# Thirty-six short extra products on TensorE ahead of weight chunks of the feed-forward layers

## The reference

```python
x = x + 0.5 * g1 * swiglu(modulate(x, sh1, sc1), ffn1_gate[l], ffn1_up[l], ffn1_down[l])
x = x + g2 * token_mix(modulate(x, sh2, sc2), ...)          # two kinds of attention
x = x + 0.5 * g3 * swiglu(modulate(x, sh3, sc3), ffn2_gate[l], ffn2_up[l], ffn2_down[l])
# swiglu(u) = (silu(u @ w_gate) * (u @ w_up)) @ w_down, width D_FF = 2816 = 22 * 128
```

## Time and profile before

| | us |
|---|---|
| median of 3 runs | 2264.29 |
| lowest and highest run | 2263.94, 2271.13 |
| span of the profiled execution, first to last instruction | 2258.5 |
| median less that span | 5.8 |
| TensorE (PE) busy | 2177.8 |
| VectorE (DVE) busy | 1526.8 |
| ScalarE (ACT) busy | 1182.8 |

### The profile page before, as it was taken

How to read it: one execution, slowest core, us unless ns; L and a number is a source line. 1 busy time by engine, 2 the same in 40 slices (tenths; PEclk the granted TensorE clock), 3 DMA queues, 4 the chain that set the end, 5 groups by cost and what they waited for, 6 DMA issues and landing times.

```text
span 2258.5 us, 40704 instructions
## 1 busy us (share of the span) xinstructions
PE 2177.8 (96%) x16754; PEld 1932.4 (86%) x16754; DVE 1526.8 (68%) x2122; ACT 1182.8 (52%) x2059; POOL 369.9 (16%) x360
## 2 busy tenths in 40 slices
PE   7999999999999999999999999999999988999998
PEld 7888988988888889988888988788878978868887
DVE  6897767688778866767775874387557544626753
ACT  4554557565455544765554664365446431526542
POOL 0111022111102100311111103020232350303001
PEclk9999999999999999999999999999998999999999
DMA  7887662467768768434665443355524300434552
GB/s 277 328 308 252 242 244 94 149 236 259 243 232 295 274 214 315 161 103 165 214 223 186 166 159 130 131 170 186 177 91 150 103 4 12 160 129 146 190 186 95
DMA packets 114232, 417.79 MB, mean 185 GB/s; under 512 B 12672, under 2 KB 12928, under 8 KB 113664
## 3 DMA queue, kind: packets, MB, share of 16 engines
q1 hardware_dynamic: 113184, 410.34, 52.2%
q10 hardware_dynamic: 864, 4.84, 0.6%
HBM read 414.09 MB, written 1.05 MB: 184 GB/s over the span
## 4 chain that ended last, share of the span: by engine, by line
PE 81%; DVE 7%; ACT 5%; issue 4%; POOL 1%; DMA 1%; POOLq 0%; SPq 0%; DVEq 0%; ACTq 0%
PE banks L551 80%; DVE weight_lower L1520 1%; DVE weight_ring L1531 1%; POOL heap L2718 1%; ACT weight_upper L2230 1%; ACT xn_t L2354 1%; PE banks L954 1%; PE banks L1340 0%; DMA weight_ring<-w_ada_dram 0%; ACT L2264 0%; ACT xn_t L2277 0%; DMA weight_ring<-w_in_dram 0%; ACT heap L2387 0%; DMA weight_ring<-ffn_up_dram 0%; ACT xn_halves L2245 0%
## 5 line engine op out<-in xcount | busy, mean ns | idle before, releaser
L551 PE MATMUL banks<-xn_halves,weight_upper 128*128 128x512 f32 (+1 forms) x3680 | 1004.8, 344 | 11.3 <-DVE weight_lower L1520 8.1
L1520 DVE TENSOR_TENSOR weight_lower<-weight_ring,weight_upper 128x1024 fp32r<-128x1024 f32 x580 | 743.1, 1287 | 315.4 <-ACT weight_upper L2230 314.2
L551 PE MATMUL banks<-xn_halves,weight_lower 128*128 128x256 f32 x2832 | 802.0, 283 | 6.6 <-DVE xn_halves L1553 2.9
L2230 ACT ACTIVATE weight_upper<-weight_ring 128x1024 fp32r<-128x1024 f32 x580 | 607.9, 1054 | 351.7 <-PE banks L551 202.6
L551 PEld LDWEIGHTS banks<-xn_halves,weight_upper 128*128 128x128 f32 x3680 | 637.6, 190 | 99.5 <-issue 7.9
L551 PEld LDWEIGHTS banks<-xn_halves,weight_lower 128*128 128x128 f32 x2832 | 538.6, 190 | 9.9 <-DVE xn_halves L1553 3.2
L551 PE MATMUL banks<-hidden,weight_upper 128*128 128x512 f32 x1216 | 430.0, 397 | 0.0
L551 PE MATMUL banks<-hidden,weight_lower 128*128 128x256 f32 x1216 | 341.7, 281 | 0.0
L551 PEld LDWEIGHTS banks<-hidden,weight_upper 128*128 128x128 f32 x1216 | 228.6, 188 | 56.4
L2718 POOL TENSOR_TENSOR heap<-heap 128x256 f32<-128x256 f32 x120 | 122.0, 1021 | 930.5 <-ACT heap L2460 614.5
L551 PEld LDWEIGHTS banks<-hidden,weight_lower 128*128 128x128 f32 x1216 | 228.2, 188 | 0.0
(11 more groups left out here) (299 smaller groups left out, 2496.1 us busy)
## 6 DMA issues: line engine op xcount, KB each, us to landing
weight_ring<-w_ada_dram SPq DMA_DIRECT2D x144, 512.0 KB, 4.5
weight_ring<-ffn_gate_dram SPq DMA_DIRECT2D x88, 512.0 KB, 3.8
weight_ring<-ffn_up_dram SPq DMA_DIRECT2D x88, 512.0 KB, 4.5
weight_ring<-ffn_down_dram SPq DMA_DIRECT2D x88, 512.0 KB, 3.4
weight_ring<-m_w_up_dram SPq DMA_DIRECT2D x64, 512.0 KB, 3.2
weight_ring<-m_w_down_dram SPq DMA_DIRECT2D x64, 512.0 KB, 3.2
weight_ring<-w_in_dram SPq DMA_DIRECT2D x58, 512.0 KB, 4.0
weight_ring<-b_w_rkv_dram SPq DMA_DIRECT2D x24, 512.0 KB, 3.2
```

The lines of the kernel that those rows point to most:

```text
L551: return nc.tensor.matmul(o, w, r, start=first, stop=last)
L1520: V.tensor_tensor(w_lo[:, n % RING, :], ring[:, n % RING, :], w_hi[:, j % SPLITS, :].bitcast(F32), ALU.subtract).then_inc(*did("weight_low ...
L2230: A.activation(w_hi[:, j % SPLITS, :], ring[:, n % RING, :], ACT.Copy).then_inc(*did("weight_upper", j))
```

## The change

In stages 2 and 5, ahead of the gate chunk of `f` = 4, 7, 10, 13, 16 and 19, and in the way down of all four feed-forward stages, ahead of chunks 4, 7, 10, 13, 16 and 19, TensorE gets an extra product (in one case two) into PSUM bank 5, whose result nobody reads. Its kind varies from place to place. It stands behind the chunk's wait in `cut` and ahead of the chunk's first pair. Nothing else is changed, and all that the kernel computed before it still computes.

```diff
+NUDGES = {(2, 4): "narrow", (2, 7): "tile", (2, 10): "two", (2, 13): "split", (2, 16): "short", (2, 19): "wide",
+          (5, 4): "half", (5, 7): "quarter", (5, 10): "turn", (5, 13): "wide", (5, 16): "narrow", (5, 19): "split"}
+DOWN_NUDGES = {4: "narrow", 7: "tile", 10: "split", 13: "turn", 16: "wide", 19: "short"}
...
+            def nudge(kind, w):
+
+                refill(5)
+                if kind == "narrow":
+                    mm(cols(5, 1), ident, ident[:, 0:1], True, True)
+                elif kind == "tile":
+                    mm(cols(5, P), ident, ident, True, True)
+                elif kind == "two":
+                    for _ in range(2):
+                        mm(cols(5, P), ident, ident, True, True)
+                elif kind == "half":
+                    mm(cols(5, 64), ident, ident[:, 0:64], True, True)
+                elif kind == "quarter":
+                    mm(cols(5, 32), ident, ident[:, 0:32], True, True)
+                elif kind == "turn":
+                    nc.tensor.transpose(cols(5, P), ident, ident)
+                elif kind == "split":
+                    mm(cols(5), w[0][:, 0:P], xn_hl[0][:, 0, :], True, True)
+                elif kind == "short":
+                    mm(cols(5, P), w[0][:, 0:P], xn_hl[0][:, 0, 0:P], True, True)
+                elif kind == "wide":
+                    mm(bank[:, 5, :].rearrange("p (h t) -> p h t", h=2), w[0][:, 0:P], xn_hl.both[:, :, 0, :],
+                       True, True)
...
-            def project_wide(name, i, x, done, readers_of, b):
+            def project_wide(name, i, x, done, readers_of, b, kind=None):
...
                 w, *used = cut(name, i)
+                nudge(kind, w)
                 for k in range(KD):
...
                             wc, *used = cut(name, i0 + m // TILES)
+                            if kt == KF and m // TILES in DOWN_NUDGES:
+                                nudge(DOWN_NUDGES[m // TILES], wc)
...
-                        project_wide(name, i, xn_hl, done, readers_of, b)
+                        project_wide(name, i, xn_hl, done, readers_of, b,
+                                     NUDGES.get((s, f)) if name.endswith("gate") else None)
```

## The result

The changed kernel takes 2272.14 us, median of 18 runs, beside 2264.01 for the kernel before in 18 runs of the same sets. The recorded ratio of the two is 1.0044, 95% interval [1.0031, 1.0058]: slower by 9.9 us, between 7.0 and 13.1. (It is not the quotient of the medians; these differ by 8.1 us, and the means by 9.6.) The forecast was 2267.3 within 2261 to 2274, that is 3.0 us slower. The time lies in the range; the loss is three times the forecast one, and it fell to the case of slower by over 0.3%, which had 0.19.

What follows compares the result with a forecast made beforehand. TensorE, running without a stop, was taken to bound the kernel. Products cost 4.9 us, quicker gate stretches return 1.9, net 3.0 more: span 2261.5, plus 5.8 to the median, 2267.3 us, range 2261 to 2274.

Steps and rivals of the forecast that it cites:

- the case of slower by over 0.3%: Whole kernel: a loss above 0.3%, 6.8 us; chance 0.19.
- What bounds the kernel: Stretches concerned: TensorE runs without a stop, so each nanosecond more or less on it is one of the kernel.
- The sum of the prices: All 36 places, 37 products: 0.91 us in stage 2, 0.80 in stage 5, 3.2 in four ways down; together 4.9 us.
- That the columns do not matter: Extra float32 products: 1 and 128 columns both cost 0.11 us; "short" taken at 0.11 too.
- Half of the gate stretches turn: Gates of stages 2 and 5: half of twelve stretches between places go to the quick rhythm, giving back 1.9 us.
- the entry seems to belong to the stage's own code: Stages 2 and 5: their like slow rhythm, 600 us apart, comes from the code, not the microsecond of entry.
- Rival D: Stage 3 and the second model's two quick stages turn slow: 5.7 us more, time 2273.0; chance 0.07.
- The ways down do not turn: Four ways down: products reading `hidden` stay at 397/397/398 ns between places, so no gain is taken there.
- Rival B: All 36 places: each breaks the overlap of weight load and product, 8.5 us more, time 2272.8; chance 0.10.
- a price of 0.2 us or more a place: Starts around a place in the profile after: the sign that broken overlap of weight load and product is right.
- my case: Some gate stretches turn quick, ways down do not: 3.0 us more, 2267.3, own range 2265 to 2269; chance 0.52.
- The 5.8 us from span to median: Whole kernel: 5.8 us added to the forecast span of 2261.5 to reach the forecast time, 2267.3.

Runs made afterwards that it cites:

- gates only: Changed kernel with the extra products in the four ways down removed, leaving the twelve gate places of stages 2 and 5: 2262.95 us, ratio 1.0005 to the kernel before.
- all "turn": Changed kernel with one transpose of the identity at each of the 36 places in place of its own kind: 2267.39 us, ratio 1.0019 to the kernel before.
- all "tile": Changed kernel with one plain float32 matmul of 128 columns at each of the 36 places: 2273.75 us, ratio 1.0059 to the kernel before.
- late block: Kernel before, plus 28 filler matmuls (6.2 us) in one block inside the program's last way down: 2268.57 us, ratio 1.0025.
- waits only: Changed kernel whose places keep their wait for bank 5 but issue no product: 2263.06 us, ratio 1.0008 to the kernel before.
- lumping: Changed kernel with the same 37 products, all of a stage's at its first place, 6 interruptions for 36: 2271.00 us, ratio 1.0043 to the kernel before.
- early block: Kernel before, plus 28 filler matmuls (6.2 us) in one block inside the way down of stage 0: 2275.18 us, ratio 1.0056.

## Why the prediction came out as it did

**What bounds the kernel: right.** TensorE hardly waits in the stretches concerned (0.4 us once in stage 2), and the products' time passed into the kernel's time whole.

**The sum of the prices: 4.9 forecast, 6.2 measured.** The mis-sized term is 0.11 us for narrow, tile, half, quarter and turn alike. It holds for the transpose, from which I read it. For the plain float32 matmul it is 0.22. The step that failed is the reading of the fillers, six in 0.66 us: the code behind these six records is `hold(7, 3)`, three matmuls. I counted records and priced instructions. With 15 such matmuls this is 1.65 us too little, of which the prices measured elsewhere give back 0.3 ("split" 0.10 and not 0.12, "wide" 0.22 and not 0.24). The four passes that the Trainium skill states ("FP8 and Floating Point Precision", TensorE Precision Notes), by which I estimated 0.21 us for 128 columns and which I set aside because "The rows show 0.11 us for exactly this product", come close to the 0.22 measured at 128 columns; but one column costs 0.22 as well, and that is not what passes of columns alone would give.

**That the columns do not matter: right** for the plain float32 kinds, and "short" costs 0.11 like "split", as taken.

**Half of the gate stretches turn: the fraction came out, what it is worth was wrong.** In the three profiles with these very places (the changed kernel twice and gates only) 18 of 36 stretches were quick. That it came to just half is partly luck: it hangs on the mix of kinds, since all "turn" gave 9 of 12 and all "tile" 4 of 12. And the gain was reckoned against stretches that are always slow, from one execution. Over the twelve profiles with pairs in the old order, stages 2 and 5 were entered quick 9 times in 24. Against that, half is worth (0.50 - 0.375) x 3.8 = 0.5 us, not 1.9. My argument that "the entry seems to belong to the stage's own code" rested on two stages of one execution and is false. Rival D, which it served to weaken, is an ordinary draw on both sides: stage 3, which D names, ran slow but for its first pairs in the changed kernel's first profile and quick in its second, and slow in the same way with the late block, whose code up to there is that of before. Stage 0, which has no added product in its gates, ran slow in the changed kernel's first profile and in the one with waits only.

**The ways down do not turn: right.** Whatever the kind, they read 397 as median in every profile in the old order.

**Rival B (a place costs over 0.19 us by breaking the overlap): its mechanism wrong.** Places with one record of up to 256 columns cost 0.10 to 0.12; those at 0.22 have two records or 512 columns; and lumping saved nothing. By the prediction's own sign, "a price of 0.2 us or more a place", B would have passed for right at the places of one plain float32 matmul. That its 2272.8 us lies beside the measured 2272.14 is luck.

**What was in no case of mine** is the rest, 3 to 4 us, that came with a lower mean clock. With the sizes put right, my case ends at 6.2 - 0.5 = 5.7 us; the late block, which is 6.2 us of products and no turn of rhythm, measured 1.0025, 5.7 us (2.9 to 8.4), so the products' own time accounts for it. The early block, with the same own time, measured 1.0056. The two blocks show that where the time is added matters. That the changed kernel's rest is of the same kind is inferred from the like mean clocks (0.9855 and 0.9850, early block 0.9857). By the estimate of 16 us for each 0.01, the 0.0021 of clock between the blocks are worth 3.4 of the 7 us between them. Why the clock is lower, in which stages the time goes, and what the other half is, stays open.

**The 5.8 us from span to median: two things in one.** In every run that lists both, the time is 1.8 to 2.0 us above that run's own span. So the profiled execution took an estimated 2260.3 us, and 4.0 of the 5.8 are its distance from the median. Since the median of 18 runs of the kernel before, 2264.01, lies beside the 2264.29 that the forecast started from, this did no harm.

## What to carry to other kernels

Before a price is read off a group of records, match the count of records to the code that issued them: one matmul of plain float32 is two records here, one transpose is one. A rhythm that one profile shows is a draw until a second profile shows it too; a second profile of the same code might have told that stages 2 and 5 are not slow as such (of the two profiles with no extra product before stage 5, waits only entered it slow, the late block quick). The same holds for the clock of a window: 0.92 stood in the profile of a slower kernel and in that of the fastest alike. And where a stream runs in two rhythms, look at the order of the stream before disturbing it: grouping equal lengths by two gave 14 us, disturbing cost 10. The order was tried for the whole stream of pairs at once, so its parts are not priced one by one.

## What was not expected of the hardware

- 6.2 us of filler products cost 1.0056 (mean clock 0.9857) near the start of the program and 1.0025 (0.9878) near its end. The reason is not shown.
- A plain float32 matmul of one column takes as long as one of 128 columns, 0.22 us, and is two records in the trace; a float32 transpose of 128 columns is one, 0.10 to 0.12 us; an fp32r one of 256 columns takes 0.10 to 0.12.
- The same stream of pairs, 512 and 256 columns by turns, runs at 347 or at 353 ns a pair for hundreds of pairs, differing from one execution to another at the same entry; out of `hidden` always at 353; in groups of two at 346 to 348 from either.
